# Operand tiles of 288 columns laid end to end, 16 bytes past a multiple of 128

## Time and profile before

| | |
|---|---|
| median of the runs | 2319.65 us |
| span of the profiled execution, first to last instruction | 2318.2 us |
| what the median has beyond that span | 1.45 us |
| TensorE matmul busy | 2301.9 us, 99% |
| DVE, ACT, POOL busy | 1419.4, 882.9, 1702.8 us |
| mean granted clock of TensorE | 0.997 |
| DMA | 458.25 MB, mean 198 GB/s |

### The profile page before, as it was taken

One profiled execution on the slowest core, in us unless ns is written; L12 is line 12 of the kernel. 1 busy time (PEld: TensorE's weight loads), 2 busy tenths in 40 slices (PEclk: granted clock), 3 DMA queues, 4 the chain that ended last, 5 costly groups with the idle time before them and its releaser, 6 DMA issues.

```text
span 2318.2 us, 48204 instructions
## 1 busy us (share of the span) xinstructions
PE 2301.9 (99%) x17575; PEld 2293.4 (99%) x17575; DVE 1419.4 (61%) x2373; ACT 882.9 (38%) x1109; POOL 1702.8 (73%) x702
## 2 busy tenths in 40 slices
PE   9999999999999999999999999999999999999997
PEld 9999999999999999999999999999999999999997
DVE  3974564355569954656565640766666777666655
ACT  5444453345544443333333333333333333333334
POOL 4876677776677777677676767777777778777775
PEclk9999999999999999999999999999999999999998
DMA  7564446654455555666666668766666666666643
GB/s 255 168 200 146 145 143 206 213 173 154 146 164 194 185 191 184 217 215 211 211 209 213 208 216 257 282 205 206 209 215 220 217 213 206 208 206 217 199 164 114
DMA packets 141275, 458.25 MB, mean 198 GB/s; under 512 B 14448, under 2 KB 37232, under 8 KB 140656
## 3 DMA queue, kind: packets, MB, share of 16 engines
q1 hardware_dynamic: 116944, 416.42, 55.6%
q10 hardware_dynamic: 24264, 40.93, 4.8%
HBM read 416.40 MB, written 43.28 MB: 198 GB/s over the span
## 4 chain that ended last, share of the span: by engine, by line
PE 95%; DVE 4%; ACT 0%; issue 0%; ACTq 0%; DVEq 0%
PE ps L1412 30%; PE ps L1413 30%; PE ps L1418 30%; PE ps L1700 1%; DVE F L1010 1%; PE ps L1453 1%; DVE F L1011 1%; PE ps L1626 1%; PE ps L1645 0%; DVE b_lo L1024 0%; PE ps L1460 0%; DVE R L1039 0%; DVE R L1073 0%; PE ps L615 0%; ACT R L964 0%; PE ps L1551 0%
## 5 line engine op out<-in xcount | busy, mean ns | idle before, releaser
L707 POOL TENSOR_TENSOR w_lo<-raw,w_hi 128x1024 fp32r<-128x1024 f32 x692 | 1694.3, 2470 | 599.4 <-ACT w_hi L734 568.4
L734 ACT ACTIVATE w_hi<-raw 128x1024 fp32r<-128x1024 f32 x690 | 692.8, 1052 | 686.1 <-PE ps L1418 652.5
L1412 PE MATMUL ps<-a_hi,w_hi 128*128 128x288 f32 x3072 | 824.8, 295 | 0.0
L1413 PE MATMUL ps<-a_lo,w_hi 128*128 128x288 f32 x3072 | 822.6, 294 | 0.0
L1412 PE MATMUL ps<-b_hi,w_hi 128*128 128x288 f32 (+1 forms) x2432 | 655.1, 295 | 0.4 <-ACT w_hi L734 0.4
L1413 PE MATMUL ps<-b_lo,w_hi 128*128 128x288 f32 (+1 forms) x2432 | 653.0, 295 | 0.0
L1412 PEld LDWEIGHTS ps<-a_hi,w_hi 128*128 128x128 f32 x3072 | 577.7, 188 | 2.4 <-issue 2.2
L1413 PEld LDWEIGHTS ps<-a_lo,w_hi 128*128 128x128 f32 x3072 | 577.9, 188 | 0.1
L1418 PE MATMUL ps<-a_hi,w_lo 128*128 128x288 f32 x3072 | 467.2, 294 | 0.0
L1412 PEld LDWEIGHTS ps<-b_hi,w_hi 128*128 128x128 f32 x2432 | 457.1, 188 | 0.9 <-issue 0.8
L1413 PEld LDWEIGHTS ps<-b_lo,w_hi 128*128 128x128 f32 x2432 | 457.8, 188 | 0.1
(11 more groups left out here) (238 smaller groups left out, 1256.4 us busy)
## 6 DMA issues: line engine op xcount, KB each, us to landing
raw<-in_peer_u SPq DMA_DIRECT2D x256, 512.0 KB, 4.3
raw<-in_peer_v SPq DMA_DIRECT2D x256, 512.0 KB, 4.0
raw<-in_w_in SPq DMA_DIRECT2D x96, 512.0 KB, 3.9
gelu_scratch<-F ACTq DMA_DIRECT2D x32, 576.0 KB, 5.7
gate_scratch<-g_stage ACTq DMA_DIRECT2D x36, 512.0 KB, 6.0
F<-gelu_scratch SPq DMA_DIRECT2D x32, 576.0 KB, 5.7
raw<-in_w_out SPq DMA_DIRECT2D x32, 512.0 KB, 3.7
raw<-in_w_query SPq DMA_DIRECT2D x32, 512.0 KB, 3.7
```

Of the source, the lines that this page charges most:

```text
L707: pool.tensor_tensor(wl[:, j, s], raw[:, j, s], wh[:, j, s].bitcast(F32), ALU.subtract).then_inc(lo_ready, 1)
L734: act.activation(wh[:, k, s], raw[:, k, s], ACT.Copy).then_inc(hi_ready, 1)
L1412: pe.matmul(out, w, mh(k), start=(n == 0), stop=False)
L1413: pe.matmul(out, w, ml(k), start=False, stop=False)
```

## The change

The operands a_hi and a_lo become one run of 16 x 288 floats, without the four floats between tiles, that begins 4 floats into the buffer. The buffer ends with 60 unused floats, so it is as large as before and all that is allocated behind it stays in place. For the gated values of peer_v, b_hi and b_lo get a second view, `vh` and `vl`: again 16 x 288 floats without gaps, beginning 20 floats into the buffer. The pooled values, the attention output and the queries' operand still use `bh` and `bl` with rows of 292.

```diff
+SHIFT, PAST_END = 4, 60
+V_HI, V_LO = 20, 20
...
-        ah, al = (sb(name, [P, KT, T + 4], F32R)[:, :, 0:T] for name in ("a_hi", "a_lo"))
+        ah, al = (sb(name, [P, SHIFT + KT * T + PAST_END], F32R)[:, SHIFT:SHIFT + KT * T].rearrange(
+            "p (k t) -> p k t", k=KT) for name in ("a_hi", "a_lo"))
...
+        vh, vl = (t[:, :, :].rearrange("p k t -> p (k t)")[:, off:off + KT * T].rearrange("p (k t) -> p k t", k=KT)
+                  for t, off in ((bh, V_HI), (bl, V_LO)))
...
-                link(ve.tensor_copy(bh[:, 8 * s + e, 0:T], AB[:, s, e, :]))
-                ve.tensor_tensor(bl[:, 8 * s + e, 0:T], AB[:, s, e, :], bh[:, 8 * s + e, 0:T].bitcast(F32),
+                link(ve.tensor_copy(vh[:, 8 * s + e, :], AB[:, s, e, :]))
+                ve.tensor_tensor(vl[:, 8 * s + e, :], AB[:, s, e, :], vh[:, 8 * s + e, :].bitcast(F32),
                                  ALU.subtract).then_inc(act_ready, 1)
...
                 pairs("peer_v", 16 * i + 8 * s, j,
-                      lambda k: bh[:, 8 * s + k, 0:T], lambda k: bl[:, 8 * s + k, 0:T], first=2)
+                      lambda k: vh[:, 8 * s + k, :], lambda k: vl[:, 8 * s + k, :], first=2)
...
-                    pairs("peer_v", 112 + 2 * n, j, a_op(bh), a_op(bl), first=2)
+                    pairs("peer_v", 112 + 2 * n, j, a_op(vh), a_op(vl), first=2)
```

More of the change, by code:

```diff
@@ L208, in layer @@
             pass
-        F = sb("F", [P, (212863 - 4 * (6 * KT * P + KT * T + 2 * KT * (T + 4) + 2 * KT * TW + VECS + CONSTS + P)) // 4 - 32])
+        F = sb("F", [P, (212863 - 4 * (6 * KT * P + KT * T + 2 * (KT * T + SHIFT + PAST_END) + 2 * KT * TW + VECS + CONSTS + P)) // 4 - 32])
         def carve(off, *shape):
```

## The result

The changed kernel takes 2337.54 us (median, 2337.36 to 2337.55) against 2319.63 us, a ratio of 1.0077 (95% interval 1.0065 to 1.0089): slower by 17.9 us. The forecast was 2293 us; the time also lies 3.5 us above the range that went up to 2334, near the 2340 us of the rival "slower".

What follows compares the result with a forecast made beforehand. TensorE, full and waiting for nobody, was taken to bound the kernel. 15,552 multiplies x 1.7 ns = 26.4 us gained; 2318.2 - 26.4 + 1.45 = 2293 us, range 2246 to 2334.

Steps and rivals of the forecast that it cites:

- rival "slower": Touched multiplies: entering a tile at place 16 costs extra, now paid each time; 1.3 ns more, 20 us, 2340 us; chance 0.20.
- What bounds the kernel, and where the change acts: TensorE is busy 2301.9 of 2318.2 us; 15,552 multiplies on a and gated values are touched, other stages unchanged.
- What one place costs: Multiplies in `product`: steps averaged by tile start within 128 bytes; place 16 lowest at 130.1, giving 1.7 ns gain each.
- step = own part + next part: Fit to the old trace's steps: place 16 has own part 62.0, next part 68.2, sum 130.2 ns against 131.9.
- the eight sums: Fitted same-place steps, places 0 to 112 by 16: 130.5, 130.2, 132.6, 133.2, 132.5, 133.2, 130.4, 132.3 ns.
- The second way to the number: Old trace, high-to-low pairs of one tile: four at place 16 average 130.05 ns, the 28 others 132.4.
- The uncertainty of 0.9 ns: On the fitted sum for place 16: single positions scatter by 2.2 ns, twelve positions carry each part.
- the shortest of thousands is 127: Lower bound for a multiply's step, from the 289 row: 127 ns, -76 us.
- all steps short: Touched multiplies: with one place everywhere each step may settle at 127 to 128.5 ns; 68 us less, 2251; chance 0.15.
- The steps did not become flat: Touched multiplies: the pattern of steps should become flat, with tiles alike; no size given.
- The rule of 16-byte lines: SBUF reads: going to a new 16-byte line too often costs; all starts are multiples of 16, so 2319.7 us.
- no effect: Touched multiplies: short and long steps may be two sides of one account; 2318 to 2321, central 2319.7 us; chance 0.14.

Runs made afterwards that it cites:

- columns_256: Against the kernel with only operand a dense (gated values in old rows): peer_u and peer_v multiplies stream 256 of 288 columns; 2174.02 us, ratio 0.9366.

## Why the prediction was wrong

- *What bounds the kernel, and where the change acts*: right. Of the stages only those with touched multiplies moved, the untouched ones stayed within 0.1 us, and no other engine came into it. One small slip: peer_u's 132.2 ns before still has 1.9 us of transposes in it; without them it is 131.9, as in peer_v.
- *"What one place costs"*: here it failed. "So I fitted step = own part + next part", with 130.2 for place 16, was the term of the sum; it measured 133.1 in both stages. The sign of the whole forecast hung on it. That place 16 had the lowest mean (130.1) was true of the old layout, and still no property of the place: its twelve positions already ran from 126.7 to 137.4 ns (the 289 and the 298 of tile 13 in the earlier trace rows). In the dense layout tile 13 times its high part takes 295 instead of 289, and of the eight sums five missed by 0.9 to 2.9 ns in one operand or both (0, 16, 48, 96, 112; 80 by 0.6).
- *The second way to the number*, the four pairs "times hi, times lo" at 130.05, was no second way: it used the same start times, and in the changed kernel the eight such steps of a peer_v product take 131.7 to 138.4 ns, on average 133.4.
- *The uncertainty of 0.9 ns* counted scatter as noise. It was not noise, since each position repeats within 0.5 ns; it was a pattern whose short and long steps belong together. A mean over the positions at one place cuts that pattern up. Sums over whole products are steadier, 131.6 to 132.1 in the trace of before; but they too are prices of one layout in one order, since the same rows in other orders gave 132.2 and 132.9. The bound "the shortest of thousands is 127" was a little high as well: some 200 of 14,900 steps take 125 or 126.
- *The rival "all steps short"*: that a dense stream "may settle" was right as a picture, since some settle in short cycles. But only a short value was thought of, and dear ones proved to be the rule: all sixteen dense stages in natural order with the weights in place, low parts moved or not, lie at 132.1 or above. The steps did not become flat either, as I had expected.
- *The rival "slower"* had the size (1.3 ns, 2340 us; measured 1.2) right, and the reason not: entering place 16 is not what is paid, since tiles all at place 0, 32 or 80 cost about as much or more. That the time came near this rival's is luck.
- *The rule of 16-byte lines* (the Trainium skill, SBUF — State Buffer, "Door 1: The DMA port swizzle"), read as "no effect", fails: places that are all multiples of 16 span 132.1 to 135.1 ns. For starts off such a multiple, rows of 289 to 291 have 133.4 to 133.6, which agrees with it in sign but is no proof.

What stays open: why a stream of 288-column multiplies falls into one cycle or another. Shown are four things that have a part in it: the operand's place, the order of tiles, the length of the read, and the move of the weights (or of the buffers that moved by 256 bytes with them). What in the chip the cycle of four multiplies stands for was not settled, and a separate stream of multiplies without anything else running wasn't tried. Nor was the same place within 128 bytes tried at another address above it, or the order of the operand's tiles apart from that of the weight tiles.

## What to carry to other kernels

When TensorE is full and waits for nobody, the layout of its operands alone can move the step of a multiply, here from 131.2 to 135.1 ns at 288 columns, the kernel's time from 0.5% less to 1.1% more; and order and layout have to be tried together, since the same order gained 1.9 ns in one layout and lost 0.9 in the other. Don't price a layout by sorting single multiplies of another layout; run it, and read whole products or stages. Stage windows in one run can test two layouts at once, once it is shown that each stage answers to its own operand.

## What the runs showed of the hardware

- Start-to-start times of TensorE multiplies of 288 columns repeat to a nanosecond in hundreds of products, with DMA, DVE, ACT and POOL busy beside them, and yet scatter from 127 to 144 ns within a product, in cycles of four (143, 139, 132, 132), two (129, 131) or more.
- Beyond the columns' 120 ns, a multiply of 288 columns took 11.2 to 15.1 ns here, and in `columns_256` one of 256 columns took 11.1 to 11.5 beyond 106.7. In both the amount differs with the layout. Halving the columns of the weight tile took 1.1 to 1.3 ns off the step.
- Rows of 289 to 291 floats, with half to three quarters of the starts off a multiple of 16 bytes, were no better than dense ones at place 16: 133.4 to 133.6 ns against 133.1.
